# Second scan: the queries' reading of the state moved from before the value products to behind them

## What is computed

```
def gdn_chunk_scan(q, k, v, beta, log_a, s0, c):
    ...
    def step(s, inp):
        q_c, k_c, u_c, w_c, a_c, tot = inp
        v_new = u_c - jnp.einsum('bhid,bhdv->bhiv', w_c, s)
        o = jnp.einsum('bhid,bhdv->bhiv', q_c, s) + jnp.einsum('bhij,bhjv->bhiv', a_c, v_new)
        s = s * tot[..., None, None] + jnp.einsum('bhid,bhiv->bhdv', k_c, v_new)
        return s, o
...
o = rms_norm(o, head_norm) * jax.nn.silu(z.astype(f32))
return o.reshape(b, l, GDN_V).astype(h.dtype) @ w_out
```

## Time and profile before

| | |
|---|---|
| time, median of 3 runs | 1404.92 us (1404.87 to 1409.62) |
| time of the profiled execution | 1404.08 us |
| its span in the trace | 1402.1 us |
| PE busy | 1381.8 us, 99% of the span |
| DVE, ACT, POOL busy | 777.3, 448.6, 413.1 us |
| scan, chunk 0's K to the last chunk's end | about 1048 to 1373 us of the span |

### The profile page before, as it was taken

The page is one execution under the profiler, slowest core; times in us unless marked ns, Lnnn a source line. Parts: engine busy times, 40 slices in busy tenths (PEclk is TensorE's granted clock), DMA queues, the critical chain, the costliest instruction groups (busy, mean ns, idle before and its releaser), DMA issues.

```text
span 1402.1 us, 20664 instructions
## 1 busy us (share of the span) xinstructions
PE 1381.8 (99%) x8181; PEld 1168.2 (83%) x8181; DVE 777.3 (55%) x921; ACT 448.6 (32%) x822; POOL 413.1 (29%) x362
## 2 busy tenths in 40 slices
PE   7999999999999999999999999999999999999998
PEld 6878799978888889999999999888877777777776
DVE  5224622234445348766666798899944654444442
ACT  5333731133222224343344533322124522211121
POOL 3122043442111112222222278223443622122200
PEclk9999999999999999999999999999999999999999
DMA  5621244475555235465566556444369966545530
GB/s 170 206 92 53 74 127 141 148 246 200 188 172 187 62 81 119 112 147 121 116 162 168 92 97 118 94 120 137 89 222 287 288 186 180 154 146 152 159 91 30
DMA packets 291322, 201.02 MB, mean 143 GB/s; under 512 B 165289, under 2 KB 254457, under 8 KB 290962
## 3 DMA queue, kind: packets, MB, share of 16 engines
q1 hardware_dynamic: 284642, 188.26, 48.4%
q10 hardware_dynamic: 6592, 11.54, 2.9%
HBM read 131.93 MB, written 67.82 MB: 142 GB/s over the span
## 4 chain that ended last, share of the span: by engine, by line
PE 62%; issue 0%; ACT 0%; POOL 0%; ACTq 0%; DVE 0%; DVEq 0%; POOLq 0%
PE banks L2190 25%; PE banks L3001 13%; PE banks L2253 12%; PE banks L3057 2%; PE banks L3090 2%; PE banks L3062 2%; PE banks L3071 1%; PE banks L3045 1%; PE banks L2140 1%; PE banks L3014 1%; PE banks L1830 1%; POOL gdn L2463 0%; ACTq L2116 0%; PE banks L3032 0%; ACT gdn L2443 0%
## 5 line engine op out<-in xcount | busy, mean ns | idle before, releaser
L2190 PE MATMUL banks<-hn_hi,gdn 128*128 128x352 f32 x1488 | 291.9, 322 | 0.0
L2190 PEld LDWEIGHTS banks<-hn_hi,gdn 128*128 128x128 f32 x1488 | 244.7, 188 | 3.1 <-issue 2.7
L2511 DVE SCALAR_TENSOR_TENSOR gdn<-gdn,conv_taps,gdn 128x1040 f32<-128x1040 f32 x96 | 168.3, 1754 | 33.3 <-ACT gdn L2317 30.4
L2190 PE MATMUL banks<-hn_lo,gdn 128*128 128x352 f32 x744 | 167.7, 320 | 0.0
L2253 PE MATMUL banks<-gdn,hn_hi 128*128 128x512 f32 x512 | 162.3, 396 | 2.2 <-POOL gdn L2463 1.7
L2456 POOL TENSOR_TENSOR gdn<-gdn,gdn 128x1024 fp32r<-128x1024 f32 x31 | 90.1, 2908 | 231.3 <-ACT gdn L2292 231.3
L2190 PEld LDWEIGHTS banks<-hn_lo,gdn 128*128 128x128 f32 x744 | 126.0, 188 | 0.0
L920 PE MATMUL banks<-gdn,hn_hi 128*128 128x512 f32 x384 | 120.7, 395 | 0.0
L2253 PEld LDWEIGHTS banks<-gdn,hn_hi 128*128 128x128 f32 x512 | 95.7, 188 | 28.2 <-issue 5.8
L2253 PE MATMUL banks<-gdn,hn_lo 128*128 128x512 f32 x256 | 101.1, 395 | 0.0
L3001 PE MATMUL banks<-gdn,gdn 128*128 128x512 f32 x384 | 95.3, 397 | 0.3
(11 more groups left out here) (317 smaller groups left out, 2302.3 us busy)
## 6 DMA issues: line engine op xcount, KB each, us to landing
gdn<-in_gdn_w_in SPq DMA_DIRECT2D x32, 512.0 KB, 4.2
gdn_v<-gdn SPq DMA_DIRECT2D x64, 132.0 KB, 4.1
gdn<-in_x SPq DMA_DIRECT2D x16, 512.0 KB, 4.0
gdn<-in_gla_w_in SPq DMA_DIRECT2D x32, 256.0 KB, 4.3
gdn_kq<-gdn SPq DMA_DIRECT2D x16, 512.0 KB, 4.0
gdn<-in_gdn_w_in SPq DMA_DIRECT2D x32, 256.0 KB, 4.0
gdn<-gdn_kq SPq DMA_DIRECT2D x16, 512.0 KB, 3.8
gdn<-gdn_ek SPq DMA_DIRECT2D x16, 512.0 KB, 6.0
```

The costliest lines, as they stand in the source:

```text
L2190: return pe.matmul(acc[n % 2][:, b, 0:m], w[n % 2][:, kt, :], x[:, kt, PAD + s:PAD + s + m], start=(kt == 0 and e == 0), stop=(kt == KT - ...
L2511: dve.scalar_tensor_tensor(cv[:, :], xs[:, tap:tap + L], T.cw[:, tap, t:t + 1], cv[:, :], ALU.mult, ALU.add).then_inc(S("ni_conv"), 1)
```

## The change

Q moves from its place behind K to one behind V, and its wait for `ns_og` goes with it. The filling that stood behind V moves ahead of V. In chunks 0 and 1, 22 and 18 products now stand between K (with T) and V, and none behind V. In later chunks it is 8 in even and 12 in odd ones, and in odd chunks `rest` grows from 32 to 36. Their total for two chunks stays 96. The program's instructions are the same in number and kind, and the order on DVE, ACT, POOL and SP is unchanged.

```diff
@@ -3036,8 +3036,8 @@
             def plan(m):
 
                 if m < 2:
-                    return ((14, 8, 40), (8, 10, 38))[m]
-                return ((0, 8, 40), (8, 8, 32))[m % 2]
+                    return ((22, 0, 40), (18, 0, 38))[m]
+                return ((8, 0, 40), (12, 0, 36))[m % 2]
 
             def read_out(m):
 
@@ -3051,16 +3051,10 @@
                 after_x, after_v, rest = plan(m)
                 pe.wait_ge(S("ns_kqd"), m + 1)
                 pe.wait_ge(S("ns_su"), 8 * m + 8)
-                wait(pe, S("ns_og"), HP * m)
                 for hp, p, q in pairs():
                     hd = 2 * hp + p
                     mm = pe.matmul(pK[R[p], hp, :], kq[m % 2][:, hd, p, :], St[:, hd, :], start=(hp % 2 == 0), stop=True,
                                    skip_group_check=True)
-                mm.then_inc(S("ns_x"), 1)
-                for hp, p, q in pairs():
-                    hd = 2 * hp + p
-                    mm = pe.matmul(pQ[R[1 - p], hp, :], kq[m % 2][:, hd, 1 - p, :], St[:, hd, :], start=(hp % 2 == 0),
-                                   stop=False, skip_group_check=True)
                 mm.then_inc(S("ns_x"), 1)
                 if j == 0 and m >= 2:
                     outputs(m - 1)
@@ -3071,6 +3065,12 @@
                     mm = pe.matmul(pK[R[q], hp, :], ua[m % 2][R[p], hp, 0, :], v[R[p], hp, :],
                                    start=(hp % 2 == 0), stop=True, skip_group_check=True)
                 mm.then_inc(S("ns_v"), 1)
+                wait(pe, S("ns_og"), HP * m)
+                for hp, p, q in pairs():
+                    hd = 2 * hp + p
+                    mm = pe.matmul(pQ[R[1 - p], hp, :], kq[m % 2][:, hd, 1 - p, :], St[:, hd, :], start=(hp % 2 == 0),
+                                   stop=False, skip_group_check=True)
+                mm.then_inc(S("ns_x"), 1)
                 if m == NCH - 1:
                     outputs(m - 1)
                 fill(after_v)
```

## The result

| | before | after |
|---|---|---|
| median of 6 runs each | 1404.89 us (1403.39 to 1409.62) | 1414.31 us (1413.29 to 1417.45) |
| ratio | | 1.0070, 95% interval 1.0055 to 1.0084 |
| time of the profiled execution | 1404.08 us | 1417.45 us |
| its span | 1402.1 us | 1415.5 us |

The change makes the kernel slower by 0.7%, 9.8 us by the ratio. The prediction was 1416.7 us, with a range of 1411.5 to 1420.0. Its mean granted clock is 0.995, that of the five others 0.997 or 0.998. So the spans differ by 13.4 us, more than the medians do.

A forecast was written before the change was run, and what follows sets the result against it. PE was taken as the bound, busy 99% of the span. Terms 7.5 + 2.6 + 1.2 + 0.3 + 0.2 = 11.8 us on 1404.08 gave 1415.9, plus 0.84 for the median 1416.7 us; range 1411.5 to 1420.0.

The forecast's parts named there:

- One of the signs that the prediction had named for being wrong: In the scan: the prediction is wrong if the granted clock reads under 1.00 there.
- An odd chunk is worth 0: Odd chunks and chunk 0: K and Q apart +0.21 us, filling in one block -0.22, four seams before and after.
- The rival in which the seams inside V, Q and DS go away: Weights load during the preceding step, 30 seams vanish at 0.20 us each, -6.0 us, giving 1410.7; chance 0.07.
- An even chunk costs 1.25: Chunks 4 to 14: first filling product waits for T's low part, no longer hidden by V; +7.5 us for six.
- Chunk 2 costs 2.6: Chunk 2: ACT turns late to T after the last z tile, so DS starts at 1103.2 instead of 1100.55 us.
- the fall of the clock: Rival, six even chunks and chunk 2: PE's stalls drop the clock to 1.2 GHz, 7 times 13, 1429.7 us; chance 0.03.
- the row that the forecast leaned on: Profile row before the change: after 1.72 us without a product the granted clock reads 1.00, cited against the clock falling.
- Chunk 1 costs 1.2: Chunk 1: filling products wait for ACT to take out z tiles 4 and 5; +1.2 us, bounds 0 to 1.5.
- Chunk 3 costs 0.3: Chunk 3: its values' load starts about 4.5 us later behind the same backlog; +0.3 us, bounds 0 and 1.5.
- Chunk 15 costs 0.2: Chunk 15, the last: Q stands between V and T, one seam more; +0.2 us.

The follow-up runs named there:

- the two experiments with seams: Kernel before with V directly behind Q in chunk 0 and odd chunks from 3, 1407.33 us; with 4 filling products between K and Q in odd chunks, 1407.75 us.
- chunk 1 alone: Kernel before with the new order only in chunk 1, 18 products in one block ahead of V; 1404.95 us, ratio 0.9989.
- the wait taken away: Changed kernel, but in even chunks from 2 on the 8 filling products between T and V move behind RO; 1407.05 us, ratio 1.0015 to the kernel before.
- the even chunks from 4 on: Kernel before with the new order only in even chunks 4 to 14; 1412.87 us, ratio 1.0057.

## Why the prediction was right

The sign and the place are as forecast, and 1414.31 lies in the range, 2.4 us under the forecast. The mechanism that decides, the filling product that waits for T's low part, is the one that the experiments show. One of the signs that the prediction had named for being wrong did appear: the clock read under 1.00 in the scan.

- **An odd chunk is worth 0.** It measured -0.06 to -0.09. K and Q apart cost 1.88 each for the 1.91 taken. The seams are dealt out anew, and the two experiments with seams put the price of one at 0.24 and 0.19. The rival in which the seams inside V, Q and DS go away is refuted by the idle times of 0.39 and 0.38 ahead of Q and DS. The Trainium skill, "TensorE: Matmul & The Clock Gate", section "Step-by-step: what each phase is for", allows the weight load ahead when row groups don't conflict or it goes to the background buffer. No load was pulled ahead across a change of form here.
- **An even chunk costs 1.25.** It measured 1.16 to 1.18 in four chunks. T to filling was 2.16 for 2.15 forecast. The idle time in it was 1.07 and not 1.2 to 1.5, since T alone took 1.09 and not 0.9; the sum didn't use either. The two chunks with 1.32 have their `rest` filling at 9.52 us instead of 9.37 for the same 40 products. Both values also occur in the other kernels of this study, 0.15 us apart, and the cause stays open.
- **Chunk 2 costs 2.6.** The stall alone is right, 2.4 in the kernel that has only this and 3.0 in the changed one. The forecast gave the fall of the clock a chance of 0.03, because 1.72 us of idle time had left the clock alone. In the profiled execution the stall was 2.56 us and the clock fell, for 2.7 us more, which the sum had at nothing. This rival was priced for seven chunks and it struck in the one chunk for which the text had named it open. The six stalls of 1.07 us left the clock at 1.00. But the row that the forecast leaned on was no safe ground: at that same place, ahead of the scan, the clock fell in the profile after the change, behind 1.83 us (last section). One execution had shown no fall, and that didn't exclude one in the next.
- **Chunk 1 costs 1.2.** The place was right and the size too large: 0.74 in the profile after and 0.97 with chunk 1 alone, but 4.2 with the wait taken away, where the clock fell too. The step that failed took ACT to be busy until 1074.61. In the profile after, ACT began with the weight row 0.8 us earlier and took out z tile 4 from 1074.06 on. The term depends on a landing time, and the bound of 1.5 was too low.
- **Chunk 3 costs 0.3.** It cost nothing: the load started 7 us later than before, 1108.98 for 1102.06, but K of chunk 3 came 6.4 later too, and the values were there. The prediction saw the wait for the values but not that it can strike the old order as well, as it did with chunk 1 alone.
- **Chunk 15 costs 0.2.** It measured 0.14.

Added up, the terms are 11.8 us. The profile has 7.3 for the six even chunks, 3.0 for chunk 2 without the fall of the clock, 0.74 for chunk 1, 0.14 for chunk 15 and -0.5 for the odd ones and chunk 0, together 10.7. The fall adds 2.7, which makes the 13.4 of the spans. The ratio says 9.8, with an interval of 7.7 to 11.8. So the sum is about 1 us too large against the profile, and part of the agreement is luck: the fall of the clock, which can add 2 to 3 us, left the median in the range because it doesn't strike as hard in every execution.

The chances were added up a little off: by the prediction's own split slower has 0.915, within 0.5% 0.075 and faster 0.01, where it gives 0.90, 0.08 and 0.02. Nothing hangs on that.

## What to carry to other kernels

Work that fills a gap is only free if it doesn't itself wait for what was just started: before moving filling, look up the waits inside it, and count what the step that stood in between was covering. On an engine that runs in order, such a wait holds up everything behind it, here V, Q and DS, though none of these needed the awaited result. And a step's distance from the one before it is also the cover of its loads: an order that was shorter in each other odd chunk lost in the one whose load landed late, so mend the load first.

## What the runs showed of the hardware

Idle stretches of PE of nearly the same length did different things to its clock. With 2.56, 2.37 and 3.57 us without a product the granted clock fell to 0.50 (0.55 over the first 2 us in the second case). By the stretches it was low for 3.4 us in the second case and 6.8 in the others. With 2.41 and 3.08 us it stayed at 1.00, and with the six stalls of 1.07 too. Shorter stalls aren't safe either. The one ahead of the scan, in the earlier trace rows 1.72 us long with a clock of 1.00, looks like this after the change:

```profile
1035.92 0.70 PE L2253 MATMUL banks<-gdn,hn_hi 128*128 128x512 f32 x2 [1.83 <-POOL gdn L2463]
```

```profile
1036.00:1038.00 2.00, 2.00 (x7) 1.61 (x8) 0.00 (x0) 0.77 (x2) 1.92 (x2) 0.78 0.75 237
1038.00:1040.00 2.00, 2.00 (x6) 1.34 (x4) 0.00 (x0) 0.60 (x1) 1.93 (x1) 0.50 0.84 274
```

With chunk 1 alone it was 1.89 us, and the clock fell to 0.56 over the stretch from 1036 to 1038. With the even chunks from 4 on it was 1.84 us, and the clock stayed:

```profile
1036.09 0.70 PE L2253 MATMUL banks<-gdn,hn_hi 128*128 128x512 f32 x2 [1.84 <-POOL gdn L2463]
```

```profile
1036.00:1038.00 2.00, 1.91 (x9) 1.61 (x10) 0.00 (x0) 0.94 (x2) 1.90 (x2) 1.00 0.81 251
```

PE's order up to there is the same in all these kernels. From the product behind this stall to K of chunk 0 it is 12.41 us in the changed kernel (1048.33 - 1035.92) and 10.92 before (1048.35 - 1037.43), so this fall cost 1.5 us. The table by chunks doesn't show it, because the stall of the kernel before ended 1.5 us later.

The Trainium skill, "TensorE: Matmul & The Clock Gate", section "Why this matters for your kernels", warns of idle gaps between bursts of products. The runs agree that a gap can do it and show that the same gap need not in the next execution. A fall cost 1.5 us ahead of the scan, 1.9 in chunk 1 (26.23 less 22.00 and the stall of 2.37), 2.7 in chunk 2 and 2.9 in chunk 3 (26.40 less 19.97 and 3.57), so a stall of this length has a price that differs from run to run.

A change of product form costs PE about 0.2 us, start to start, at each boundary, though the list of waits shows 0.33 to 0.39 us of idle time of the weight load there: the rest of that idle time lies under the products that are still running, as Q in chunk 5 after the change, busy until 1166.52 + 1.95 = 1168.47 by the profile with DS starting at 1168.40.
